# Writing the residual sum with adding DMA transfers from GpSimd's queue at the end of the expert stage

## The reference

```
    x = x + gt1 * (merged @ w_out[l])                      # called h in the kernel: the residual
    h2 = _rms(x, g_ffn[l]).astype(x.dtype) * (1.0 + sc2) + sh2
    x = x + gt2 * moe_ffn(h2, ...)                         # the result
```

## Time and profile before

| what | value |
|---|---|
| median of 3 runs | 1505.45 us |
| lowest and highest run | 1503.59 and 1507.17 us |
| span of the profiled execution | 1502.7 us |
| time of the profiled execution outside its span | not given by the profile |
| TensorE (PE) busy | 96% of the span |
| VectorE busy | 66% |
| ScalarE busy | 53% |
| GpSimd busy | 6% |

### The profile page before, as it was taken

How to read it: one execution, slowest core, us unless ns; L and a number is a source line. 1 busy time by engine, 2 the same in 40 slices (tenths; PEclk the granted TensorE clock), 3 DMA queues, 4 the chain that set the end, 5 groups by cost and what they waited for, 6 DMA issues and landing times.

```text
span 1502.7 us, 38731 instructions
## 1 busy us (share of the span) xinstructions
PE 1443.4 (96%) x16045; PEld 1176.9 (78%) x16045; DVE 985.2 (66%) x1386; ACT 791.7 (53%) x1015; POOL 96.0 (6%) x57
## 2 busy tenths in 40 slices
PE   7999799999999999999999899989999999999998
PEld 6997667999999989999898899866565555555554
DVE  4597443367665457764654755587888778788786
ACT  5446226244333358634233455457676666767674
POOL 1200300002332000000210000010000000000000
PEclk9999999999999999999999999999999999999999
DMA  9667277555555535543124244399999999999995
GB/s 311 188 199 228 83 252 249 173 162 178 174 189 176 191 112 169 167 143 113 59 86 140 86 149 168 104 378 367 415 413 367 417 415 415 415 415 409 416 415 195
DMA packets 179172, 364.40 MB, mean 242 GB/s; under 512 B 9293, under 2 KB 137786, under 8 KB 162234
## 3 DMA queue, kind: packets, MB, share of 16 engines
q1 hardware_dynamic: 179002, 362.00, 66.4%
HBM read 356.08 MB, written 2.10 MB: 238 GB/s over the span
## 4 chain that ended last, share of the span: by engine, by line
PE 76%; DVE 5%; DMA 4%; ACT 3%; issue 2%; DVEq 0%; SPq 0%; ACTq 0%; POOLq 0%
PE psum L3432 12%; PE psum L375 9%; PE psum L376 8%; PE psum L379 8%; PE psum L3448 6%; PE psum L3403 4%; DMA proj<-in_w_exp_up 3%; PE psum L3485 3%; PE psum L707 3%; PE psum L572 3%; PE psum L508 2%; PE psum L509 2%; PE psum L510 2%; PE psum L550 2%; DVE ring L2619 1%
## 5 line engine op out<-in xcount | busy, mean ns | idle before, releaser
L375 PE MATMUL psum<-proj_r 128*128 128x256 f32 x1392 | 341.6, 286 | 3.9 <-ACT proj_r L339 3.9
L376 PE MATMUL psum<-proj_r 128*128 128x256 f32 x1392 | 339.0, 284 | 0.0
L344 DVE TENSOR_TENSOR ring_r<-ring,proj_r 128x2048 fp32r<-128x2048 f32 x94 | 223.7, 2380 | 154.3 <-ACT proj_r L339 153.7
L2619 DVE COPY ring<-proj 128x1024 f32 x374 | 236.5, 687 | 82.1 <-PE psum L3432 55.1
L375 PEld LDWEIGHTS psum<-proj_r 128*128 128x128 f32 x1392 | 268.0, 193 | 8.3 <-issue 7.3
L376 PEld LDWEIGHTS psum<-proj_r 128*128 128x128 f32 x1392 | 268.1, 193 | 0.1
L339 ACT ACTIVATE proj_r<-ring 128x2048 fp32r<-128x2048 f32 x93 | 177.5, 1909 | 103.4 <-PE psum L379 93.0
L1952 ACT ACTIVATE ring<-proj 128x1024 f32 x186 | 189.0, 1051 | 6.2 <-issue 4.5
L379 PE MATMUL psum<-proj_r,ring_r 128*128 128x256 f32 x1392 | 181.2, 283 | 0.0
L379 PEld LDWEIGHTS psum<-proj_r,ring_r 128*128 128x128 f32 x1392 | 173.3, 192 | 0.1
L3432 PE MATMUL psum<-ring,work 128*32 128x256 f32 x1536 | 116.8, 381 | 0.7 <-ACT work L1922 0.7
(11 more groups left out here) (573 smaller groups left out, 2612.6 us busy)
## 6 DMA issues: line engine op xcount, KB each, us to landing
ring<-in_w_in SPq DMA_DIRECT2D x65, 1024.0 KB, 5.3
proj<-in_w_exp_gate SPq DMA_DIRECT2D x64, 1024.0 KB, 9.8
proj<-in_w_exp_up SPq DMA_DIRECT2D x64, 1024.0 KB, 11.2
proj<-in_w_exp_down SPq DMA_DIRECT2D x64, 1024.0 KB, 12.0
ring<-in_w_ada SPq DMA_DIRECT2D x24, 1024.0 KB, 9.0
ring<-in_w_ffn_in SPq DMA_DIRECT2D x22, 1024.0 KB, 5.1
ring<-in_w_ffn_out SPq DMA_DIRECT2D x11, 1024.0 KB, 4.9
ring<-in_w_out SPq DMA_DIRECT2D x8, 1024.0 KB, 5.2
```

The lines of the kernel that those rows point to most:

```text
L344: dve.tensor_tensor(ring_r[:, at.slot, :], ring[:, at.slot, :], self.heads[at.buffer].bitcast(F32), ALU.subtract) \
L375: pe.matmul(dst, w, xh, start=start, stop=False, skip_group_check=True)
L376: pe.matmul(dst, w, xl, start=False, stop=False, skip_group_check=True)
L2619: ins = dve.tensor_copy(into_copy[k_half][j][:, kind * D:(kind + 1) * D], pieces[:, bass.ds((piece + kind) % PIECES, 1), of_half].rearrang ...
```

## The change

The residual is not read back. It stays in `out`, where SP stored it, and the four quarters of `out_tok` are sent there by DMAs that add to what they find (`accum_op=ALU.add`). They are issued from GpSimd's queue, each when its product by the gain is ready, in the order (b, n) = (0,0), (1,0), (0,1), (1,1). The two adds on GpSimd and the two on VectorE are gone, as are SP's two loads and its four writes; SP keeps the last wait for all four transfers.

```diff
@@ GROUPS_OF_SIGNALS
-    "tiles_moved": [("input_heads_moved", 16), ("input_rests_moved", 16), ("h_kept", 32), ("h_returned", 32)],
+    "tiles_moved": [("input_heads_moved", 16), ("input_rests_moved", 16), ("h_kept", 32)],
@@ views
-        h_back = pieces[:, (3 * EXPERTS + 1) % PIECES, :].rearrange("p (b d) -> p b d", b=TB)
@@ SP
                 sp.dma_start(dst, src).then_inc(sig(f"piece_loaded_{at % PIECES}"), 16)
-            sp.wait_ge(*reached("h_kept", 32))
-            last = EXPERTS - PIECES // 3
-            ended = sp.value_load(ends_of[:, last:last + 1], min_val=1, max_val=BLOCKS)
-            sp.wait_ge(*reached("into_copied", ended * 2 + (ended & 1)))
-            for b in range(TB):
-                sp.dma_start(h_back[:, b, :], out[0, b * P:(b + 1) * P]).then_inc(sig("h_returned"), 16)
-            for b, n in ((0, 0), (1, 0), (1, 1), (0, 1)):
-                at = slice(n * 512, n * 512 + 512)
-                sp.wait_ge(*reached(f"out_ready_{b}_{n}", 1))
-                sp.dma_start(out[0, b * P:(b + 1) * P, at], out_tok[:, b, at]).then_inc(sig("out_written"), 16)
             sp.wait_ge(*reached("out_written", 64))
@@ GpSimd
-            for b in range(TB):
-                pool.wait_ge(*reached("moe_scaled", b + 1))
-                pool.wait_ge(*reached("h_returned", 32))
-                pool.tensor_tensor(out_tok[:, b, 0:512], out_tok[:, b, 0:512], h_back[:, b, 0:512], ALU.add).then_inc(sig(f"out_ready_{b}_0"), 1)
+            pool.wait_ge(*reached("h_kept", 32))
+            for n in range(2):
+                for b in range(TB):
+                    at = slice(n * 512, n * 512 + 512)
+                    pool.wait_ge(*reached("moe_scaled", 2 * n + b + 1))
+                    pool.dma_start(out[0, b * P:(b + 1) * P, at], out_tok[:, b, at], accum_op=ALU.add).then_inc(sig("out_written"), 16)
@@ VectorE
-            for b in (1, 0):
-                dve.wait_ge(*reached("moe_scaled", 3 + b))
-                dve.wait_ge(*reached("h_returned", 32))
-                dve.tensor_tensor(out_tok[:, b, 512:D], out_tok[:, b, 512:D], h_back[:, b, 512:D], ALU.add).then_inc(sig(f"out_ready_{b}_1"), 1)
```

## The result

Over 6 runs each, the changed kernel takes 1512.91 us (median; 1510.85 to 1514.29) against 1505.14 (1502.50 to 1507.31). The ratio is 1.0050, with a 95% interval of 1.0034 to 1.0065: slower by 5.1 to 9.8 us. The change makes the kernel about 0.4% slower.

What follows compares the result with a forecast made beforehand. TensorE, busy 96%, was taken to bound the kernel, then a serial tail; issues ending at 1500.95 plus 3.52 gave 1504.47 against 1502.7, +1.8 on the median 1505.45, so 1507.2 us; range 1503.6 to 1512.0.

Steps and rivals of the forecast that it cites:

- My sum: Program's tail: last issue ends at 1500.95, plus 3.52 us behind it, gives 1504.47 against 1502.7, +1.8 us.
- The read-back is worth 0: Residual's two loads before the tail: removing them brings weights earlier, but 3.8 us of cover makes that worth nothing.
- My sign for the rest: Ahead of the tail: TensorE's part up to the last sum should stay at 1495.1 within a few tenths.
- The removal of the adds gives 1.87: Tail between last product and last write: without the four adds the last issue could start 1.87 us earlier.
- The issues, 1.27 each: GpSimd's four issues in the tail: 1.27 us each, from its add of 128x512, the first starting at 1495.87.
- The queue, not the data, sets the pace: GpSimd's issues in the tail: the second to fourth products are ready before their turn, so the issues' queue sets the pace.
- My term for adding: Behind the last issue: a plain write's 2.81 us plus one more pass of data, 0.71, makes 3.52.
- 3.5 (mine), over 4.8 (B): Sign, last issue's end to span's end: 2.8 us means adding is free, 3.5 the forecast, over 4.8 slow adding at memory.
- rival B: Adding slow at memory: 8.0 us behind the last issue, 1511.7, or engines full at three times the data time; chance 0.25.
- Rival A: Tail: GpSimd's issues cost near SP's 0.35 us, so the adds' time is won, -1.9 us, 1503.6; chance 0.2.
- Rival C: GpSimd's issues in the tail are slow, 2.54 us each, or have a first-use cost: +6.8 us, 1512.3; chance 0.1.
- The estimate from the page: Transfers on GpSimd's path: about 2.0 us plus bytes at 436 GB/s, 2.6 for 256 KB, making the change 2 us faster.

Runs made afterwards that it cites:

- plain_by_sp: The changed kernel with four plain writes issued by SP instead of GpSimd's adding transfers, residual left out; ratio to before 0.9986, tail 5.3 us.
- plain_by_pool: The changed kernel with plain writes instead of adding ones from GpSimd's queue, residual left out; ratio to before 0.9995, tail 6.9 us.
- room4096: The changed kernel with dynamic_dma_scratch_size=4096 instead of 1024, more room for GpSimd's descriptors; ratio to before 1.0024, tail 11.6 us.
- room1152: The changed kernel with dynamic_dma_scratch_size=1152 instead of 1024; one run, 1505.57 us, only its profile read, tail 10.95 us.
- eighths: The changed kernel, 1024 bytes of room, with eight adding transfers of 64 rows instead of four of 128; one run, 1509.76 us, tail 15.3 us.

## Why the prediction was wrong

The tail's growth, as differences between the profiles: the adds leave (plain_by_sp against before), -2.3; the issues move to GpSimd (plain_by_pool against plain_by_sp), +1.7; the transfers add (room4096 against plain_by_pool), +4.7; the room is too small (changed against room4096), +1.6. That makes +5.7, against 13.2 - 7.6 = 5.6. Each term comes from single executions; with room1152 in room4096's place the last two are 4.0 and 2.3.

My sum had a tail of 1504.47 - 1495.10 = 9.4 us. Against it the changed kernel's 13.2 is 3.8 more: the last issue ends 0.8 earlier than in my sum when there is room (5.0 behind the first product's start in room4096, 5.85 in mine), what follows it takes 3.1 more (6.6 instead of 3.52), and the missing room adds 1.6; the three round to 3.9. So the issues, priced too high, hid a part of what the adding was priced too low.

*The read-back is worth 0.* Right, as far as profiles show it. Windows of 7 us before and in the changed kernel, the second 1.6 later like its tail:

```profile
1478.00:1485.00 7.00, 6.28 (x90) 3.81 (x86) 5.82 (x10) 5.84 (x8) 0.00 (x0) 1.00 0.83 302
1479.60:1486.60 7.00, 6.28 (x90) 3.80 (x86) 5.82 (x10) 5.83 (x8) 0.00 (x0) 1.00 0.42 153
```

The DMA share halves, as the prediction said, and TensorE does the same 90 instructions in the same 6.28 us. No run undoes this part by itself. My sign for the rest, TensorE's part ending within a few tenths of 1495.1, could not be read: the first product starts at 1496.71 and 1495.60 in two executions of the same changed kernel.

*The removal of the adds gives 1.87.* Right in kind; it measured 2.3.

*The issues, 1.27 each.* With room enough the pace is 3.70 / 4 = 0.93 us, for plain ones 2.31 / 4 = 0.58. I took too much, and for the wrong reason: 64 rows cost nearly as much as 128 (0.86 and 0.93), so the engine's time over 128 rows was no measure of it. What I left out is a delay ahead of the first: it starts 1.33 behind the start of the first product, 0.64 behind its end, where my sum had 0.08.

*"The queue, not the data, sets the pace": this is the step that failed, in two ways.* First, with 1.8 us of data for each transfer against 0.93 of issue, the DMA engines are what the transfers queue for. My term for adding, one more pass of 0.71 us behind the last issue, let the others hide under the issues. Adding measured 1.1 us more for each of the four, 7.3 instead of 2.8 us in all, so that in room4096 the span ends 6.6 us behind the last issue's end (1501.90), where I had 3.52. In the changed kernel itself it ends 1509.9 - (1505.45 + 0.89) = 3.6 behind it, which by my own sign ("3.5 (mine), over 4.8 (B)") would speak for my term; that is luck, since its fourth transfer was issued to empty engines. My rival B had the full engines as its second form ("three times that"); it measured 2.6 times. Its first form, 8.0 us behind the last issue, did not come. Second, no step and no rival asked how many transfers GpSimd can have in flight. The wait for room put 4.6 us between the third and the fourth issue and cost 1.6 to 2.3 us of tail, less than its length because the engines were busy with the first three for most of it.

*Rival A* (cheap issues, 1503.6) fell, though the issues were cheap: even plain ones from GpSimd's queue measure no difference from before, and the adding costs 4.7 us of tail on top. *Rival C* was wrong in its size: the four issues take 3.70 us together where it had 4 x 2.54, and the start-up is 0.64.

*The estimate from the page.* The Trainium skill, "DMA: Bandwidth & Descriptors" (anatomy of one DMA), gave an estimate of 2.6 us for a transfer of 256 KB. The four of plain_by_pool landed 2.5 to 3.1 us after their issue, so for plain transfers the trace agrees; the changed kernel's adding ones took 3.8 to 5.9. The 2 us faster that I had drawn from it did not come for plain ones either: plain_by_pool's tail is 0.7 under before's.

*The range.* The median on record, 1512.91, lies 0.9 above its upper end. I had cut that end to 1512.0, under even the centre of rival C (1512.3), and no case joined two of the costs that the runs show. The forecast of +1.8 us and the 0.56 for "within 0.2%" were the real error: the larger part of it is the adding, the smaller the room.

## What to carry to other kernels

An adding DMA is not an add for free: here 256 KB cost 1.8 us of all DMA engines instead of 0.7, so at the end of this program, where nothing covers it, it was dearer than an add of 0.7 to 1.3 us on an idle engine and a plain write. Where a tail is a queue of transfers, compare one transfer's data time with the pace of the issues before deciding which of them sets the end. Before transfers move to GpSimd's queue, count what those in flight take of the room that the program reserves for their descriptors; the one that did not fit waited here until all ahead of it were through.

## What the runs showed of the hardware

- GpSimd's queue starts its first issue 0.64 us after the product that releases it (SP: 0.07) and goes on every 0.58 us for plain and every 0.93 us for adding transfers of 128 rows of 2 KB (0.86 for 64 rows, 0.95 for 128 rows of 4 KB). The products here come 0.6 apart, so a pace under that was hardly asked for.
- An adding transfer of 128 x 512 makes 144 packets (576 / 4), a plain one from the same queue 80 (320 / 4). Full, in windows of 1 us, the DMA engines moved the changed kernel's adding transfers at 160 to 188 GB/s; plain_by_pool reached 332. Both count the 256 KB of a transfer once (q0 has 1.05 MB in either run), so what an adding one reads of the output isn't in its rate.
- With 1024 bytes of room, three adding transfers of 128 rows are issued one behind the other, or seven of 64 rows; with 1152 bytes four of 128 rows. The counts of 17 and 9 entries in room1152's and eighths' expectations fit all three, if the room is counted for each DMA engine; 16 and 8 with one entry kept free fit too. The Trainium skill, "DMA: Bandwidth & Descriptors" (terms), gives a descriptor 16 bytes. These runs are consistent with that size and don't measure it by itself.
- A transfer without room waited until the engines were empty: in eighths the DMA share is 0.00 from 1503.5 and the issue starts at 1504.01, in the changed kernel from 1505.0 and at 1505.45. Whether the room comes back in one piece or is only looked at when the queue is empty, no run tells.
- GpSimd's DMA queue adds nothing around the span: 1.8 us outside it in the changed kernel, and 1498.52 - 1496.7 = 1.8 in plain_by_sp, which does not use it.
